# A transformer block pair on one core: first weights reordered, two rows spread by TensorE, one store moved, a bias table made with one product

## The reference, cut to what matters

```python
def first_block(x, c, ...):
    mod = silu(c) @ w_ada + b_ada                     # nine rows of 1024: shifts, scales, gates
    sh1, sc1, g1, sh2, sc2, g2, sh3, sc3, g3 = split(mod, 9)
    u = rmsnorm(x, norm_ff1) * (1 + sc1) + sh1
    h = x + 0.5 * g1 * (silu(u @ w_gate) * (u @ w_up)) @ w_down      # ff1, width 2816
    h = h + g2 * token_mixing(...)      # gated linear attention and block attention, with
                                        # rel_bias[:, rel_bucket(q_pos - k_pos)] on the logits
    h = h + 0.5 * g3 * swiglu(...)                                   # ff2
    return rmsnorm(h, norm_final)

def second_block(x, mem, ...):
    x = x + hybrid_mixer(rmsnorm(x, norm_mix_w), ...)                # delta rule and mLSTM
    x = x + memory_cross_attention(rmsnorm(x, norm_xa_w), rmsnorm(mem, norm_mem_w), ...)
    x = x + peer_ffn(...)               # each token gathers 128 rows of peer_u and of peer_v
    return rmsnorm(x, norm_final_w)
```

## Time and profile before

| | us |
|---|---|
| median of 3 runs | 1604.54 (1603.48 to 1606.39) |
| the profiled execution, its own time | 1605.79 |
| its span, first to last instruction | 1604.5 |
| TensorE busy | 1459.5 (91%) |
| VectorE busy | 1076.1 (67%) |
| ScalarE busy | 720.5 (45%) |
| DMA: moved, mean rate over the span | 470.69 MB, 293 GB/s |

### The profile page before, as it was taken

How to read it: one execution, slowest core, us unless ns; L and a number is a source line. 1 busy time by engine, 2 the same in 40 slices (tenths; PEclk the granted TensorE clock), 3 DMA queues, 4 the chain that set the end, 5 groups by cost and what they waited for, 6 DMA issues and landing times.

```text
span 1604.5 us, 21156 instructions
## 1 busy us (share of the span) xinstructions
PE 1459.5 (91%) x7714; PEld 1048.4 (65%) x7714; DVE 1076.1 (67%) x1995; ACT 720.5 (45%) x1575; POOL 344.8 (21%) x327
## 2 busy tenths in 40 slices
PE   6999999999999999899999989988888888888777
PEld 6899988899888888888886666444333433333222
DVE  5677875765677767658662286767777677667744
ACT  4444445464354444755331243544444444444443
POOL 0200210000010000000001034544444444444441
PEclk9999999999999999989999999999999999999999
DMA  8988885447567665433334389999999999999996
GB/s 317 350 315 308 306 324 164 153 145 269 216 194 234 217 196 195 164 122 106 119 119 165 134 348 406 421 420 420 421 422 421 421 421 421 423 421 421 421 421 253
DMA packets 91799, 470.69 MB, mean 293 GB/s; under 512 B 10864, under 2 KB 11040, under 8 KB 58160
## 3 DMA queue, kind: packets, MB, share of 16 engines
q0 software_dynamic: 40160, 284.63, 43.2%
q1 hardware_dynamic: 50688, 183.52, 33.2%
q10 hardware_dynamic: 848, 1.18, 0.2%
HBM read 462.75 MB, written 4.46 MB: 291 GB/s over the span
## 4 chain that ended last, share of the span: by engine, by line
PE 54%; DMA 27%; DVE 9%; ACT 7%; issue 3%; POOL 0%; SPq 0%; ACTq 0%; DVEq 0%; POOLq 0%
DMA Ft<-peer_uv,ids 15%; DMA u<-peer_uv,ids 8%; PE ps L1383 7%; PE ps L588 5%; PE ps L578 4%; PE ps L580 4%; PE ps L579 4%; PE ps L1203 3%; DVE Ft L2236 3%; PE ps L589 2%; PE ps L632 2%; PE ps L1286 2%; PE ps L708 2%; PE ps L634 2%; PE ps L633 2%
## 5 line engine op out<-in xcount | busy, mean ns | idle before, releaser
L1383 PE MATMUL ps<-Ft 128*128 128x512 f32 x792 | 375.9, 608 | 73.0 <-ACT Ft L2814 71.7
L2236 DVE CUSTOM_DVE_ANT_0 Ft<-Ft 128x1024 f32<-128x1024 f32 x198 | 242.9, 1227 | 150.1 <-DMA Ft<-peer_uv,ids 141.8
L1383 PEld LDWEIGHTS ps<-Ft 128*128 128x128 f32 x792 | 140.1, 190 | 289.4 <-ACT Ft L2814 168.6
L1411 DVE TENSOR_TENSOR wlo<-raw,whi 128x1024 fp32r<-128x1024 f32 x228 | 276.0, 1229 | 74.3 <-ACT whi L2260 74.0
L2951 POOL DMA_INDIRECT Ft<-peer_uv,ids x198 | 218.4, 1103 | 292.9 <-PE ps L1383 257.0
L2260 ACT ACTIVATE whi<-raw 128x1024 fp32r<-128x1024 f32 x228 | 232.4, 1050 | 30.6 <-DMA raw<-ff_gu 8.6
L2808 ACT ACTIVATE Ft<-Ft 128x1 f32<-128x1 f32 x256 | 51.9, 203 | 351.1 <-DVE Ft L2236 350.9
L578 PE MATMUL ps<-u,whi 128*128 128x256 f32 x688 | 199.6, 290 | 8.1 <-DVE wlo L1411 5.8
L579 PE MATMUL ps<-u,whi 128*128 128x256 f32 x688 | 195.9, 285 | 0.0
L580 PE MATMUL ps<-u,wlo 128*128 128x256 f32 x688 | 195.8, 285 | 0.0
L578 PEld LDWEIGHTS ps<-u,whi 128*128 128x128 f32 x688 | 133.0, 193 | 12.1 <-issue 5.9
(11 more groups left out here) (480 smaller groups left out, 2381.3 us busy)
## 6 DMA issues: line engine op xcount, KB each, us to landing
raw<-ff_gu SPq DMA_DIRECT2D x88, 512.0 KB, 4.7
raw<-w_mod SPq DMA_DIRECT2D x48, 512.0 KB, 5.5
raw<-ff_dn SPq DMA_DIRECT2D x44, 512.0 KB, 4.8
raw<-w_in SPq DMA_DIRECT2D x32, 512.0 KB, 3.7
raw<-w_in_s SPq DMA_DIRECT2D x28, 512.0 KB, 3.7
raw<-w_ada SPq DMA_DIRECT2D x24, 512.0 KB, 4.7
raw<-w_out SPq DMA_DIRECT2D x14, 512.0 KB, 4.0
raw<-w_in_m SPq DMA_DIRECT2D x12, 512.0 KB, 3.6
```

The costliest lines, as they stand in the source:

```text
L1383: ins = t.matmul(acc[r][c], diag[n % NDIAG], gbuf[SEAT[n]][:, 1024 + c * 512:1024 + (c + 1) * 512], start=False, stop=(n % 128 == 127))
L1411: v.tensor_tensor(lo, raw_slot(j), hi.bitcast(F32), ALU.subtract).then_inc(*up("lo", j))
L2236: v.tensor_tensor_reduce(pjunk, gbuf[SEAT[n]][:, 0:1024], xn[:, q // 8, :], 1.0, 0.0, ALU.mult, ALU.add, dots[:, n:n + 1]).then_inc(*up("d ...
```

## The change

Five edits. (1) The list starts with four `mod` tiles instead of a `w` tile, the two later `w` tiles are placed further back, TensorE makes all four first shifts ahead of `norm_start`, and VectorE's and ScalarE's order is rewritten to match. (2) `crow` is loaded as one row of 4 KB by ScalarE's queue, spread over 128 partitions by two TensorE products with a row of ones, and Silu reads the result from PSUM. (3) The bias table is one product with four output rows; ScalarE copies 4x512, and the store reads each of the four rows 128 times. (4) The store of the memory tokens also waits for the split of ff1's last down tile. (5) The final norm's row is loaded as 4 KB, spread by two products after pair 123, and copied by ScalarE after pair 126.

```diff
-    stream = ff1[:1] + mods[:2] + ff1[1:2] + mods[2:4] + ff1[2:3] + mods[4:]
+    stream = mods[:4] + ff1[:1] + mods[4:8] + ff1[1:2] + mods[8:10] + ff1[2:3] + mods[10:]
...
+                         (66, "cols1v"), (100, "rows", 1), (101, "ones2"), (123, "gfin"), (126, "gfina"), (137, "last", 0, 0), (145, "last", 0, 1),
...
-            for hh in range(4):
-                o = bank(("fb", hh))
-                t.matmul(o, bc(rb[0:32, hh:hh + 1], [32, 128]), oh[0:32, :], start=True,
-                         stop=True).then_inc(*up("fb_t", hh))
-                give(("fb", hh), "fb_a", hh)
+            t.matmul(bank("fb")[0:4, :], rb[0:32, 0:4], oh[0:32, :], start=True, stop=True).then_inc(*up("fb_t"))
+            give("fb", "fb_a")
+
+        def first_row():
+            o = bank("crow", 2)
+            t.wait_ge(*at("ones"))
+            t.wait_ge(*at("crow"))
+            for n in range(2):
+                ins = t.matmul(o[:, n * 512:(n + 1) * 512], ones[0:1, :], crow[0:1, n * 512:(n + 1) * 512],
+                               start=True, stop=True)
+            ins.then_inc(*up("ada_t", "crow"))
+            give("crow", "cact", "row")
...
             if which == 0:
-                for k in range(3):
+                first_row()
+                for k in range(NMOD):
                     first_shift(k)
                 norm_start(name, h, 2)
-                first_shift(3)
...
-            lows(cur.upto(0))
             v.wait_ge(*at("bcol"))
...
             gain(0)
-            lows(cur.upto(mod_at[0, 1] - 1))
             gain(1)
+            lows(cur.upto(split_at[0]))
+            gain(2)
+            gain(3)
             mean_square("ff1")
-            lows(cur.upto(mod_at[0, 2] - 1))
+            lows(cur.upto(split_at[1]))
             v.wait_ge(*at("ident"))
             scaled_identity("ff1")
-            gain(2)
+            gain(4)
+            lows(cur.upto(split_at[2]))
+            gain(5)
             low(0)
-            gain(3)
             low(1)
-            gain(4)
+            gain(6)
             low(2)
-            gain(5)
             low(3)
-            gain(6)
             low(4)
+            gain(7)
             low(5)
-            gain(7)
...
+            a.wait_ge(*at("ada_t", "crow"))
+            for n in range(2):
+                ins = a.activation(crow[:, n * 512:(n + 1) * 512], spot["crow"][:, n * 512:(n + 1) * 512], ACT.Silu)
+            ins.then_inc(*up("cact", "row"))
...
-            p.wait_ge(*at("fb_a", 3))
-            p.dma_start(skew, fb).then_inc(*land("skew"))
+            p.wait_ge(*at("fb_a"))
+            p.dma_start(bass.AP(skew.tensor, skew.offset, [(512, 4), (2048, 128), (1, 512)]),
+                        bc(fb[0:4, 0:512].unsqueeze(1), [4, 128, 512])).then_inc(*land("skew"))
...
         p.wait_ge(*at("ulo", "mem", 3))
+        p.wait_ge(*at("lo", last_down["ff1"]))
         p.dma_start(D["memory"], mem_a[:, :]).then_inc(*land("mem_out"))
...
                 p.wait_ge(*at("peer_t", "tile", 9, 1))
-                row(("gfin1", "second"), gfin2, D["norm_final_w_2"], 1024)
+                p.dma_start(gfin2[0:1, :], D["norm_final_w_2"]).then_inc(*land("gfin1", "second"))
```

More of the change, by code:

```diff
@@ L212, in peer_order @@
                          (16, "val", 1), (18, "turn", 1), (61, "cols1"), (62, "mean1"), (65, "cols1a"),
-                         (66, "cols1v"), (100, "rows", 1), (137, "last", 0, 0), (145, "last", 0, 1),
+                         (66, "cols1v"), (100, "rows", 1), (101, "ones2"), (123, "gfin"), (126, "gfina"), (137, "last", 0, 0), (145, "last", 0, 1),
                          (160, "last", 0, 2)):
@@ L1372, in peer @@
                     peer_keys(*args)
+                elif what == "gfin":
+                    o = bank("gfin", 2)
+                    t.wait_ge(*at("ones2"))
+                    t.wait_ge(*at("gfin1", "second"))
+                    for c in range(2):
+                        ins = t.matmul(o[:, c * 512:(c + 1) * 512], ones2[0:1, :], gfin2[0:1, c * 512:(c + 1) * 512],
+                                       start=True, stop=True)
+                    ins.then_inc(*up("peer_t", "gfin"))
+                    give("gfin", "peer_a", "gfin")
                 elif what == "pair":
@@ L2182, in last_norm @@
                 if r == 0:
-                    v.wait_ge(*at("gfin1", "second"))
+                    v.wait_ge(*at("peer_a", "gfin"))
                 for n in range(2):
@@ L2208, in peer @@
                         pass
+                elif what == "ones2":
+                    v.memset(ones2, 1.0).then_inc(*up("ones2"))
                 elif what == "mean0":
@@ L2332, in buckets @@
         def buckets():
-            for hh in range(4):
-                a.wait_ge(*at("fb_t", hh))
-                a.activation(fb[:, hh * 512:(hh + 1) * 512], spot["fb", hh], ACT.Copy).then_inc(*up("fb_a", hh))
+            a.wait_ge(*at("fb_t"))
+            a.activation(fb[0:4, 0:512], spot["fb"][0:4, :], ACT.Copy).then_inc(*up("fb_a"))
         def first_norm():
@@ L2352, in block @@
                 a.activation(u[0][:, k * 256:(k + 1) * 256], o, ACT.Identity, scale=g, bias=s).then_inc(*up("uhi", "ff1", k))
[L2354 to L2357 removed]
+            a.wait_ge(*at("ada_t", "crow"))
+            for n in range(2):
+                ins = a.activation(crow[:, n * 512:(n + 1) * 512], spot["crow"][:, n * 512:(n + 1) * 512], ACT.Silu)
+            ins.then_inc(*up("cact", "row"))
+            highs(cur.upto(split_at[0]))
             a.wait_ge(*at("x"))
@@ L2360, in first_norm @@
             a.wait_ge(*at("bcol"))
-            highs(cur.upto(mod_at[0, 2] - 1))
-            for k in range(8):
+            highs(cur.upto(split_at[1]))
+            shift(0)
+            highs(cur.upto(split_at[2]))
+            block(0)
+            for k in range(1, 8):
                 shift(k)
@@ L2803, in peer @@
                     choice_k(args[0])
+                elif what == "gfina":
+                    a.wait_ge(*at("peer_t", "gfin"))
+                    for c in range(2):
+                        ins = a.activation(gfin2[:, c * 512:(c + 1) * 512], spot["gfin"][:, c * 512:(c + 1) * 512], ACT.Copy)
+                    ins.then_inc(*up("peer_a", "gfin"))
                 elif what == "pair":
@@ L2876, in residual @@
                 p.tensor_tensor(hv, hv, restmp[name][:, r * 512:(r + 1) * 512], ALU.add).then_inc(*up("resp", name, r))
-        row(("crow",), crow, D["c_row"], 1024)
         p.memset(mhalf, -0.5).then_inc(*up("mhalf"))
```

7 lines of the change are left out of this document (2 added, 5 removed).

## The result

The change makes the kernel slower: 1624.25 us (median of 4, 1619.30 to 1629.28) against 1604.15 (median of 4, 1603.48 to 1606.39), ratio 1.012 with a 95% interval of 1.0095 to 1.0145. The forecast was 1594.3. The profiled execution took 1619.91, its span is 1618.6: 14.1 us more than the span before.

The account below looks back on a forecast made before the run. Up to about 940 us compute, mostly TensorE, bounds the kernel, then gathers filling the DMA engines. From 1604.5, -3.1 - 2.9 - 1.7 + 1.5 - 2.8 - 1.2 = -10.2 gives 1594.3 us, range 1589 to 1598 (chance 0.62).

Parts of the forecast that it names:

- the store to skew: Bias table's 1 MB store in ff1, now from four partitions: +1.5 us taken, bounds 0 and +7.5.
- The sign that the prediction named for being wrong: Table's store holding up ff1 by more than 5 us, or `norm_start` coming after 27.
- First stage -3.1: Kernel start: reordered loads and shifts let VectorE's last `low` end at 39.0 instead of 42.1; bounds 0 and -7.
- Memory tokens -2.8: End of ff1: later store removes TensorE's two waits of 1.70 and 1.09 us; bounds 0 and -2.8.
- Final row -1.2: Gather stretch: 512 KB fewer loaded, 0.524 MB at 421 GB/s, so -1.2 us.
- Table's products -2.9: Bias table in ff1: three of four products go, 3 x 0.97 us on TensorE, so -2.9.
- The clock -1.7: Behind the bias table's product: TensorE stays at 2.4 GHz, giving back half of 3.4 us; bounds 0 and -1.7.
- The store to skew stalls ff1: Rival: four engines carry the bias table's store and all 7.5 us come through, 1600.3 us; chance 0.14.
- Its case of four engines at full rate: Store to skew in ff1: four engines each carry 256 KB at 26.3 GB/s, 10.0 us, 7.5 more than now.
- Slower than before: Rival: the store to skew ends on two DMA engines or one, 13.3 us of waiting, 1606 us; chance 0.06.
- Its second part: Step 8: a store landing over 25 us later delays `mem` on POOL's queue, so ScalarE and all splits behind wait.
- The other three: Rivals: first stage gives nothing (1597.4), memory store still meets due tiles (1597.1), together 0.14; ff1's gain lost before gathers (1603.3), 0.04.

Follow-up runs that it names:

- third set: Twelve stores added at the end of the kernel before, from 2 to 16 partitions at various spacings; 1 MB from four adjacent landed in 44.3 us, 36 apart in 13.4.
- old table: The changed kernel with edit 3 undone (four products, four copies, store from 128 partitions): 1599.01 us, ratio 0.9947 to the kernel before.
- four partitions by 32: The kernel of the spread heads with the store reading only partitions 0, 32, 64 and 96, each 128 times: 1604.73 us, ratio 0.9985 to before.
- four by 36: The kernel of the spread heads with the store reading only partitions 0, 36, 72 and 108, each 128 times: 1594.86 us, ratio 0.993 to before.
- spread heads: The changed kernel with each head's column widened to 32, the product filling 128 partitions and the store reading each 4 times: 1593.0 us, ratio 0.9916 to before.
- the first stage alone: The kernel before with only edits 1 and 2, the first stage's new order and crow's row spread by TensorE: 1603.68 us, ratio 0.9989.
- the memory store alone: The kernel before with only the memory tokens' store moved behind the split of ff1's last down tile: 1600.16 us, ratio 0.9975.
- Four one-partition stores: The changed kernel with its 1 MB store to skew cut into four DMAs, each reading one partition 128 times: 1622.51 us, ratio 1.0098 to before.

## Why the prediction was wrong

**The step that failed is the store to skew**, "If only four of the 16 DMA engines work on it, each carries 256 KB at 421/16 = 26.3 GB/s, 10.0 us", with its +1.5 and bounds 0 and +7.5. It measured +29.6. The engines were taken to be what is short. Four of them did work: 256 packets of 616 ns are 158 us of engine time in 42.2 us, 3.7 engines (the four adjacent partitions of the third set), so here the trace agrees with the rule of the Trainium skill that the prediction named. But all four read through one port, which gives 25 GB/s to the four together: 42 us and not 10. I had bounded the cost by rows of transfers with 128 partitions and looked up only how engines are chosen, not what feeds them. The Trainium skill states it, "SBUF — State Buffer", section "Door 1: The DMA port swizzle": partitions reach the DMA engines by 16 ports, partitions 0 to 3 and 32 to 35 are one of them, and four adjacent partitions gave 27.6 GB/s there. The third set agrees on which partitions share a port, and its 24.9 GB/s is a tenth lower. By that page's figure the store of 1 MB is an estimated 38 us; its packets took 42.2. The sign that the prediction named for being wrong, ff1 held up by more than 5 us, is what came.

**How 42 us of a slow store become 30 of waiting.** The prediction said that two queues share an engine packet by packet, and for the stores from four partitions the bytes agree. DMA queues (packets, MB, share of 16 engines) from 60 to 80 us in after, with the old table and with four partitions by 32, and from 60 to 75 us with four by 36:

```profile
q1 hardware_dynamic: 676, 2.45, 40.5%
q0 software_dynamic: 263, 0.50, 22.7%
```

```profile
q1 hardware_dynamic: 1443, 5.25, 74.3%
```

```profile
q1 hardware_dynamic: 1056, 3.83, 60.3%
q0 software_dynamic: 251, 0.84, 16.0%
```

```profile
q1 hardware_dynamic: 1027, 3.77, 72.2%
q0 software_dynamic: 211, 0.79, 13.5%
```

In after an engine of the store's four carries 0.50/4 = 0.125 MB of the store (q0) and 2.45/16 = 0.15 MB of tiles (q1); by 32 it is 0.21 and 0.24, by 36 0.20 and 0.24. Nearly one to one each time: a tile's packet of 0.16 us waits for one of the store's, 0.6, 0.32 or 0.16 us long, and since every tile has packets on each engine, the four hold up all. Tiles flow at 2.45/5.25 = 0.47 of what ff1 drew with the old table; over 45.1 us that is 24 us short, where 25.8 were waited. By 32 it is 0.73 over 27.5 us: 7.4, waited 7.7. By 36 the mean rate is 0.96 of it, 3.77/15 against 5.25/20, or 1 us short; 4.5 were waited, so there the mean doesn't tell the wait. The measure taken for ff1's need matters too: with spread heads the same queue moved 6.23 MB in these 20 us and 4.45 in 15,

```profile
q1 hardware_dynamic: 1711, 6.23, 79.3%
```

and against that the same working gives 27.4, 10.6 and 3.2 us. Turns give the size of the wait for the first two within 3 us and too little for the third; what adds to them there is open.

**The rest of the sum was right in mechanism, and near in size.** First stage -3.1: its steps came as written (first `total` 9.48 for 9.8, `norm_start` 22.30 for 23.3, last `low` 39.17 for 39.0, last `mod` tiles issued by 28), and split 4 is 2.2 to 4.3 us ahead in the eight kernels that have it. Seven of these had no low clock up to there and before had 3.4 us of it, so up to 1.7 of this is clock; after, which had as much of it as before (at 32.3), is 2.2 ahead: the term was somewhat too large. One reason in it is not shown: the slow shifts and products early in the program were put down to a clock at its lower level, but the windows of before give a granted clock of 1.00 up to 35 us, and the records behind them begin at 28.3, so the level early on is not known. The durations held all the same (3.74 us for the two products, 3.5 for a shift). Memory tokens -2.8: -3.4, and `consts` and the residual behind it (254.43, on ff1's new end) cost nothing. Final row -1.2: -1.2 to -1.4; the row of 4 KB still took 15.5 us to land among the gathers, and TensorE waited 0.6 for it. Table's products -2.9: from split 4 to 10 the offset falls by 2.4 to 2.9 with one product, and by 0.2 with four. From split 68 to pair 120 the offsets move by -4.7 to +4.0 us, also in kernels that are alike there; the low clock falls at other places in each, and no cause beyond it was looked for.

**The clock -1.7** can't be put down to the products. No kernel with one product had its clock lowered between 50 and 60 us (seven traces), but of those with four products before and the old table had (59.1, 57.1), and the first stage alone and the memory store alone had not.

**The rivals.** *The store to skew stalls ff1* was the right one, with 7.5 us where it is 29.6. Its case of four engines at full rate is the kernel with 36 apart: it lost 5.7 us, between the 1.5 of the sum and the 7.5. *Slower than before* had the right consequence and the wrong cause: it asked for fewer than three engines, and about four did it. Its second part, ScalarE waiting for `mem`, did not come: `mem` was issued at 113.10, but the first square of it, at 140.16, had moved back with ff1 and waited for nothing. The other three fell: the first stage gave time, the tiles behind ff1 did not lose the memory store's 3.4 us, and with spread heads the lead of 9.7 us at split 68 is 11.4 at pair 120, so nothing was lost on the way. With the store from 128 partitions the five edits give a span of 1592.0; the forecast without its +1.5 for the store is 1592.8.

## What to carry to other kernels

Work taken off an engine may change the shape that a DMA then reads: a result on four partitions, repeated, is as many bytes as one on 128, but it came here through one port at 25 GB/s in place of over 200 (1 MB in 4.4 us from 128 partitions). Before such a change, look at which partitions the source has and how they are spaced, and not only at bytes and number of engines; if few rows are all there are, space them (36 apart cost 5.7 us where adjacent cost 29.6) or let the product make more rows, which cost next to nothing (1.12 us for the product where it had been 1.02, and one GpSimd copy of 0.47 off the path). And a slow transfer does not only come late itself: the weight tiles that shared its engines took 14 to 30 us to land in place of 5 to 7, so count what streams beside it.

## What the runs showed that was not expected

Four one-partition stores starved the tiles harder than one four-partition store (29.3 us in one wait, tiles at 0.16 MB in 20 us), though all engines shared the work; there the two queues did not go one to one (0.56 MB of the store beside 0.16), and why is left open. A DMA share of 0.99 can thus stand beside 36 GB/s: here the share counts as busy the 2.26 us that one packet of 4 KB takes. And the granted clock fell to 1.2 GHz for 10.2 and 13.7 us (from 73.3 and 93.8) in and behind the idle stretches of after, which made 25.8 us of waiting cost 29.6.
